# Token mixers with a shorter pipeline of steps, another step order, and gated keys copied by ScalarE

## The chip, the cores and the metric

The kernel runs on one core of a Trainium2 chip. The metric is the device time of one execution in microseconds; the median of three runs before the change is 2277.98 us (2274.43 to 2282.07).

## The reference

One inference step of a decoder with two layers, for a prompt of 512 tokens and for 8 samples of 8 tokens each (64 tokens), all in float32, width 1024. Per layer:

```
x += W_out @ concat(retention, gla, mlstm)(rmsnorm(x))      # 6, 6 and 4 heads, value width 64
x += memory_cross_attention(rmsnorm(x)); x += swiglu(rmsnorm(x))
# each mixer, in chunks of 128 tokens (8 for the samples):
o = (q k^T * decay) v + (q * q_decay) S ;  S = S * chunk_decay + (k * k_decay)^T v
# retention: fixed decays per head; gla: exp of a running sum of gates per channel;
# mlstm: exp of gate sums less a running maximum, and a normaliser as 65th value column
o = o * rsqrt(mean(o*o) + EPS) * gain * gate                 # per head and token
```

Every state is an output, of the prompt (starting from zero) and of the samples (starting from given states).

## The kernel before

**Units.** The large products stream weights. One unit is a block of 128 x 1024 of weights: a transfer (SyncE's queue) into `RAW`, an upper part `WH` by ScalarE (`upper`), the rest `WL` by GpSimd (`rests`), and 48 products on TensorE (`three`, L571): upper times upper, rest times upper and upper times rest, for two halves of 288 tokens and 8 blocks of the depth. The input is held so too, as `XH` and `XL`. After the output projection ("out") and after the projection of the cross attention ("xo"), `next_norm` adds each unit's sum to x (`add_to_x`, L1331), squares it, and behind the last unit writes all eight blocks of the next `XH` (ScalarE, `x_upper`) and `XL` (VectorE, `x_rest`, L1292); then come the sums of squares (L1302) and the statistics (L1308).

**The mixers.** Between the value projection and "out" stand 15 steps per layer, `STEPS`: for each chunk c of the prompt (0 to 3) and then for the samples (c = 4, written `NC` or S) the groups 0 (retention, three pairs of heads), 1 (gla, three) and 2 (mlstm, two). Step (1,2) is mlstm in chunk 1. Pairs of heads share the 128 partitions; in every prompt chunk the queries of the two heads are laid apart by ScalarE in `QE` (zero elsewhere). For step s TensorE runs `scores` (k q^T; for gla, `KG` holds keys with decays relative to four reference rows, 24 instructions of 64 columns), `keys` (transposes), `outputs` (the state's part from `QI` and `ST`, the values' part, and the new state's product into PSUM) and `back` (transposes of the normalised output). VectorE runs `mask_scores` (keys into `KTT`, scores times a mask into `SMX`), `take_outputs` (a copy of the outputs from PSUM to `OC`, L1695 and L1705), the sum of squares (L1784), the normalisation in place (L1799), `update_state` (mask the product L1718, scale the state L1727, add L1729), the gate (L1810), and for gla the decayed keys (a subtraction L1588 in `before`, a product L1602 in `before_end`). ScalarE lays queries apart, takes exponentials and squares `OC`; GpSimd makes the power -1/2 (L982, L986) and, for the samples, spreads values by sample (`own_values`, L253).

**Order.** Each engine's order is written out: TensorE in iteration i runs scores(i), back(i-3), keys(i), outputs(i-1). PSUM banks alternate by parity of the step. Engines are in order, and every hand-over is a semaphore. The states of the samples come by transfers that wait in SyncE's queue: `SC` and `SBD` (block-diagonal form) for three pairs at a time. In an `SBD` step 48 products and 12 of 512 columns stand on TensorE.

**Ahead of the steps** lies the gate arithmetic: a scan on VectorE (L1547), exponentials on ScalarE, GpSimd's clear of `QE` (L962) and its product for the decayed keys `KDG` (L965).

## Time and profile before

| | |
|---|---|
| median of 3 runs | 2277.98 us |
| profiled execution: time, span | 2289.77 us, 2287.8 us |
| mean granted clock of TensorE | 0.933 |
| mixers of layer 0, first scores to next projection | 314.5 to 475.2 us |
| mixers of layer 1 | 1437.2 to 1601.4 us |
| cross attention, feed-forward and projections | the rest, in both layers |

Times in the rows are microseconds from the start of the span, unless they are means in ns. PE is TensorE (PEld its weight loads), DVE VectorE, ACT ScalarE, POOL GpSimd.
### The profile page before, as it was taken

To read this page: it belongs to the slowest core of one execution; us is meant where nothing else is said; L and a number is where in the kernel's file an instruction comes from. 1 tells how busy PE (TensorE), PEld (TensorE's weight loads), DVE (VectorE), ACT (ScalarE), POOL (GpSimd) and SP (SyncE) were. 2 spreads that over 40 slices of the span, in tenths; PEclk is the share of its full clock that TensorE was granted. 3 is DMA by queue.
4 is the path that set the end of the run, shared out by engine and by line. 5 is a ranking of instruction groups with operands and counts; after the bars stand their busy time and mean duration, and the time that the engine had idled before them with its cause. 6 is when DMAs were issued, how large, how long until landed. Compare 5 with 4: busy or idle time off the path is not lost. (4 is left out here: it accounts for less than half of the span.)

```text
span 2287.8 us, 35847 instructions
## 1 busy us (share of the span) xinstructions
PE 2037.1 (89%) x14140; PEld 1908.2 (83%) x14140; DVE 938.2 (41%) x1301; ACT 626.3 (27%) x840; POOL 726.6 (32%) x356
## 2 busy tenths in 40 slices
PE   5999858689889999999799996786998999999995
PEld 5899647489679999999779984674994999999994
DVE  4543676624314330332173366774343243203313
ACT  4311542023323221222251126210323232212221
POOL 3333311323123334333343332122330233333331
PEclk9999967889999999999899997767999999999997
DMA  5432101225432222222343320013236122222221
GB/s 213 148 114 84 57 0 51 83 79 188 168 121 75 87 83 89 84 84 83 113 147 128 102 74 33 1 51 119 103 139 240 65 75 84 84 93 83 83 86 51
DMA packets 61270, 219.81 MB, mean 96 GB/s; under 512 B 10612, under 2 KB 11288, under 8 KB 58792
## 3 DMA queue, kind: packets, MB, share of 16 engines
q1 hardware_dynamic: 60216, 214.32, 26.1%
q10 hardware_dynamic: 880, 3.11, 0.4%
q8 instruction: 116, 1.90, 0.3%
q14 instruction: 58, 0.48, 0.1%
HBM read 202.47 MB, written 11.40 MB: 93 GB/s over the span
## 5 line engine op out<-in xcount | busy, mean ns | idle before, releaser
L954 POOL TENSOR_TENSOR WL<-RAW,WH 128x1024 fp32r<-128x1024 f32 (+1 forms) x276 | 645.1, 2337 | 1221.2 <-ACT WH L995 1221.2
L571 PE MATMUL PS<-XH,WH 128*128 128x288 f32 x2880 | 622.4, 298 | 18.4 <-DVE XL L1292 10.1
L571 PE MATMUL PS<-XH,WL 128*128 128x288 f32 x2880 | 618.9, 297 | 0.0
L571 PE MATMUL PS<-XL,WH 128*128 128x288 f32 x2880 | 618.9, 297 | 0.0
L995 ACT ACTIVATE WH<-RAW 128x1024 fp32r<-128x1024 f32 x276 | 292.3, 1059 | 1093.0 <-PE PS L571 1065.3
L571 PEld LDWEIGHTS PS<-XH,WH 128*128 128x128 f32 x2880 | 466.8, 190 | 24.1 <-issue 21.1
L571 PEld LDWEIGHTS PS<-XL,WH 128*128 128x128 f32 x2880 | 466.8, 190 | 0.0
L571 PEld LDWEIGHTS PS<-XH,WL 128*128 128x128 f32 x2880 | 466.8, 190 | 0.0
L571 PE MATMUL PS<-HH,WH 128*128 128x288 f32 x704 | 151.2, 296 | 4.1 <-DVE FT L1919 4.1
L571 PE MATMUL PS<-HH,WL 128*128 128x288 f32 x704 | 150.8, 296 | 0.0
L571 PE MATMUL PS<-HL,WH 128*128 128x288 f32 x704 | 150.7, 296 | 0.0
L1919 DVE TENSOR_TENSOR FT<-PS,RS 128x576 f32<-128x576 f32 x44 | 33.3, 758 | 235.9 <-PE PS L571 235.9
L1929 DVE TENSOR_TENSOR XT<-PS,XT 128x576 f32<-128x576 f32 x32 | 22.8, 752 | 251.5 <-PE PS L571 251.5
L571 PEld LDWEIGHTS PS<-HH,WH 128*128 128x128 f32 x704 | 113.3, 189 | 5.0 <-issue 5.0
L571 PEld LDWEIGHTS PS<-HH,WL 128*128 128x128 f32 x704 | 113.4, 189 | 0.0
L571 PEld LDWEIGHTS PS<-HL,WH 128*128 128x128 f32 x704 | 113.4, 189 | 0.0
L1926 DVE TENSOR_TENSOR HL<-FT,HH 128x576 fp32r<-128x576 f32 x44 | 93.2, 2118 | 33.3 <-ACT HH L995 33.3
L1331 DVE TENSOR_TENSOR XT<-PS,XT 128x576 f32<-128x576 f32 x32 | 24.2, 758 | 164.9 <-PE PS L571 164.9
L982 POOL TENSOR_SCALAR S<-S 128x6 f32<-128x6 f32 (+3 forms) x30 | 5.9, 198 | 213.6 <-DVE S L1784 213.6
L995 ACT ACTIVATE KTT<-OC 128x384 f32<-128x384 f32 (+3 forms) x30 | 14.6, 487 | 215.9 <-DVE OC L1695 129.5
L571 PE MATMUL PS<-MH,WH 128*128 128x256 f32 x128 | 39.6, 310 | 37.4 <-DVE ML L1345 33.5
L571 PE MATMUL PS<-QE,KT 128*128 128x256 f32 x80 | 25.0, 449 | 53.0 <-ACT QE L995 53.0
(259 smaller groups left out, 2474.7 us busy)
## 6 DMA issues: line engine op xcount, KB each, us to landing
RAW<-in_w_gu SPq DMA_DIRECT2D x88, 512.0 KB, 3.4
RAW<-in_w_dn SPq DMA_DIRECT2D x48, 512.0 KB, 3.4
RAW<-in_w_in SPq DMA_DIRECT2D x44, 512.0 KB, 3.5
KV<-in_cache_k SPq DMA_DIRECT2D x32, 512.0 KB, 7.1
KV<-in_cache_v SPq DMA_DIRECT2D x32, 512.0 KB, 7.3
RAW<-in_w_xk SPq DMA_DIRECT2D x16, 512.0 KB, 4.6
RAW<-in_w_xv SPq DMA_DIRECT2D x16, 512.0 KB, 3.4
RAW<-in_w_v SPq DMA_DIRECT2D x16, 512.0 KB, 3.4
```

The lines of the kernel that those rows point to most:

```text
L571: return nc.tensor.matmul(out, lhsT=lhsT, rhs=rhs, start=start, stop=stop)
L954: nc.gpsimd.tensor_tensor(WL[:, s, w], RAW[:, r, w], WH[:, s, w].bitcast(f32), ALU.subtract).then_inc(split_done.sem, 1)
L982: nc.gpsimd.tensor_scalar(small("ms", n, par)[0:L], small("ss", n, par)[0:L], 1.0 / 64, EPS, ALU.mult, ALU.add).then_inc(pool_step.sem, po ...
L995: return nc.scalar.activation(out, in_, func, **kw)
L1331: tt(two(XT[:, b, :]), halves(b % 2), two(XT[:, b, :]), ALU.add).then_inc(gemm_evac.sem, 1)
L1919: tt(two(FT[:, 2 + b % 2, :]), halves(1), two(RS[:, :]), ALU.mult).then_inc(gemm_evac.sem, 1)
L1926: tt(HL[:, b, :], FT[:, 2 + b % 2, :], HH[:, b, :].bitcast(f32), ALU.subtract).then_inc(hl_ready.sem, 1)
L1929: tt(two(XT[:, b, :]), halves(b % 4), two(XT[:, b, :]), ALU.add).then_inc(gemm_evac.sem, 1)
```

## The change

- **Step order.** The 15 steps run (0,0) (0,1) (1,0) (1,1) (2,0) (2,1) (3,0) (3,1) (0,2) (S,0) (1,2) (S,1) (2,2) (3,2) (S,2).
- **Shorter pipeline.** TensorE in iteration i runs scores(i+1), keys(i+1), back(i-2), the new `new_state(i)` (the state's product, taken out of `outputs`), outputs(i). `back` lies two steps behind instead of three.
- **Outputs.** No copy to `OC` first: ScalarE squares the outputs from PSUM, VectorE sums the squares (`mean_squares`, with EPS, formerly GpSimd's) before the next mask, and `take_outputs` normalises straight from PSUM. The mlstm division by the normaliser, and retention's query decay, are common factors of a row of outputs: they are left out and EPS is scaled instead (`EPSR`); retention's mask is built by ScalarE (`RD`, `RDS`) without them.
- **Retention scores** use half of the partitions per head, without `QE`. Chunk 0 has no product with the state.
- **State.** Two buffers `ST[0]`, `ST[1]`: ScalarE writes the scaled state into the other one (`scale_state`), VectorE adds the halves of the product.
- **Decayed keys.** The subtraction is gone; ScalarE takes twelve exponentials of 128 elements with the reference as bias. The transposed gated keys are copied to `KTT` by ScalarE (`take_decayed_keys`).
- **Samples.** ScalarE spreads the values (`spread_values`), GpSimd clears two query tiles `QB`.
- **Transfers.** `SC` is loaded right after the gate arithmetic, `SBD` for the first three pairs after the transposes of (3,1), for the second three after the products of (S,0), `SBDM` after those of (S,1), `SCM` after the transposes of (3,2). Their order in SyncE's queue stays otherwise; the store of the first `SC` still stands ahead of its second load.
- **Projections.** In the last unit of "out" and "xo" TensorE signals each block of `XH`/`XL` that it is done with (`x_free`), and `next_norm` writes the next one at once, seven of eight before the last sum.

The diff's core:

```diff
-STEPS = [(c, g) for c in range(NC + 1) for g in range(3)]
+STEPS = [(0, 0), (0, 1), (1, 0), (1, 1), (2, 0), (2, 1), (3, 0), (3, 1),
+         (0, 2), (NC, 0), (1, 2), (NC, 1), (2, 2), (3, 2), (NC, 2)]
+AT = {step: n for n, step in enumerate(STEPS)}
+APART = [n for n, (c, g) in enumerate(STEPS) if c < NC and g > 0]
+UNDECAYED = [n for n, (c, g) in enumerate(STEPS) if g != 1]
+SCALED = [n for n, (c, g) in enumerate(STEPS) if 0 < c < NC]
+GAMMA = [1.0 - 2.0 ** (-5.0 - h) for h in range(6)]
...
-        ST = sb("ST", [128, PAIRS, 130])
...
+        QB = [place("QB0", [128, 3, 576], r_kk), place("QB1", [128, 3, 576], r_xh)]
...
+                            if frees and b == stop - 1 and k < KB - 1:
+                                last.then_inc(x_free.sem, 1)
...
+                        if s in APART:
+                            both = bank(q + p // 2, 256 * (p % 2), 256).rearrange("p (e i) -> p e i", e=2)
+                            slot = APART.index(s) % 2
+                            if grp == 2:
+                                mm(both, KT[:, p0 + p, t0:t0 + L], QE[:, slot, p, :, :], True, True)
+                                continue
                             for i in range(4):
                                 w = slice(32 * i, 32 * i + 32)
-                                mm(both[:, :, w], KG[:, p, i, :], QE[:, s % 2, p, :, w], True, True)
-                        elif c < NC:
-                            mm(both, KT[:, p0 + p, t0:t0 + L], QE[:, s % 2, p, :, :], True, True)
-                        else:
-                            for e in range(2):
-                                r = slice(64 * e, 64 * e + 64)
-                                k = KGS[r, p, :] if grp == 1 else KT[r, p0 + p, t0:t0 + L]
-                                mm(bank(q + e, CH * p, L)[0:L], k, QT[r, p0 + p, t0:t0 + L], True, True)
+                                mm(both[:, :, w], KG[:, p, i, :], QE[:, slot, p, :, w], True, True)
+                            continue
...
+                def new_state(s):
...
+                    if c == NC:
+                        pe.wait_ge(sm_ready.sem, sm_ready.at(l, s + 1))
+                        pe.wait_ge(vb_ready.sem, vb_ready.at(l, grp + 1))
+                    stand_alone(pe)
+                    for p in range(n):
+                        if c < NC:
+                            last = mm(bank(q + 2, 2 * W * p, 2 * W), KTT[:, par, 128 * p:128 * p + 128],
+                                      V[:, c, value_at(grp, p, 0, W):value_at(grp, p, 0, W) + 2 * W], True, True)
+                            continue
+                        for e in range(2):
+                            k = KTT[0:64, par, 128 * p + 64 * e:128 * p + 64 * e + 64]
+                            last = mm(bank(q + p)[64 * e:64 * e + 64], k, own_values(grp)[:, 2 * p + e, :], True, True)
...
+                    last.then_inc(u_done.sem, 1)
...
+                        pe.wait_ge(gated.sem, gated.at(l, s - 1))
...
+                        if 0 < c < NC:
+                            queries = (QT if grp == 0 else QI)[:, p0 + p, t0:t0 + L]
+                            mm(o2, queries, state(c % 2, p0 + p, 1)[:, 0, 0:2 * W], True, False)
...
-                for i in range(len(STEPS) + 3):
+                scores(0)
+                keys(0)
+                for i in range(len(STEPS) + 2):
+                    if i + 1 < len(STEPS):
+                        scores(i + 1)
+                        keys(i + 1)
+                    if i >= 2:
+                        back(i - 2)
                     if i < len(STEPS):
-                        scores(i)
-                    if 3 <= i:
-                        back(i - 3, i)
-                    if i < len(STEPS):
-                        keys(i)
-                    if 1 <= i <= len(STEPS):
-                        outputs(i - 1)
+                        new_state(i)
+                        outputs(i)
...
+                nc.gpsimd.memset(QB[1][:, :, :], 0.0).then_inc(qb_zero.sem, 1)
...
+                nc.gpsimd.tensor_tensor(KDG[:, :, 0:SEQ], KDG[:, :, 0:SEQ], KT[:, 3:6, 0:SEQ], ALU.mult).then_inc(kdg_ready.sem, 1)
+                nc.gpsimd.tensor_tensor(KDS[:, :, :], KDG[:, :, SEQ:NT], KT[:, 3:6, SEQ:NT], ALU.mult).then_inc(kdg_ready.sem, 1)
...
-                    act.wait_ge(unit_done.sem, unit_done.at(l, U0[stage] + 8))
                     for k in range(KB - 1):
+                        act.wait_ge(x_free.sem, x_free.at(l, (KB - 1) * (n - 1) + k + 1))
                         x_upper(name, k)
-                        if k == 2:
-                            upper(stage, 7 + SPLIT_SLOTS)
+                    upper(stage, 7 + SPLIT_SLOTS)
...
+                def decay_keys(c):
+
+                    if c == 0:
+                        act.wait_ge(ga_used.sem, ga_used.at(l, 1))
+                    else:
+                        act.wait_ge(ma_done.sem, ma_done.at(l, AT[c - 1, 1] + 1))
+                    for p in range(3):
+                        for i in range(4):
+                            last = do(KG[:, p, i, :], GB[:, p, CH * c:CH * c + CH], ACT.Exp, scale=-1.0 / 16,
+                                      bias=small("gref", 1, 16 * p + 4 * c + i))
+                    last.then_inc(kg_exp.sem, 1)
...
+                def scale_state(s):
+
+                    if s in SCALED:
+                        c, grp = STEPS[s]
+                        p0, n = GROUPS[grp]
+                        act.wait_ge(st_done.sem, st_done.at(l, AT[c - 1, grp] + 1))
+                        act.wait_ge(mb_done.sem, mb_done.at(l, AT[c - 1, grp] + 1))
...
+                        for p in range(n):
...
+                            last = do(state((c + 1) % 2, p0 + p, 1)[:, 0, :], state(c % 2, p0 + p, 1)[:, 0, :], ACT.Copy, scale=decay)
+                        last.then_inc(st_scaled.sem, 1)
+
+                def take_decayed_keys(s):
+
+                    c, grp = STEPS[s]
+                    if grp == 1:
+                        L = chunk_of(c)[1]
+                        if s >= 2:
+                            act.wait_ge(u_done.sem, u_done.at(l, s - 1))
+                            act.wait_ge(ss_ready.sem, ss_ready.at(l, s - 1))
+                        act.wait_ge(ma_done.sem, ma_done.at(l, s + 1))
+                        do(KTT[0:L, s % 2, 0:384], bank(4 * (s % 2) + 2, 0, 384)[0:L], ACT.Copy).then_inc(kg_taken.sem, 1)
+
+                def spread_values(grp, half):
+
...
+                    for b in range(4 * half, 4 * half + 4):
+                        last = do(own_values(grp)[:, :, 64 * b:64 * b + 64], v, ACT.Copy,
+                                  scale=COLS[0:64, COL["batch"] + b:COL["batch"] + b + 1])
+                    if half == 1:
+                        last.then_inc(vb_ready.sem, 1)
+
+                decay_keys(0)
                 act.wait_ge(qe_zero.sem, qe_zero.at(l, 1))
                 act.wait_ge(g_ready.sem, g_ready.at(l, 1))
...
+                for i in range(len(STEPS)):
+                    c, grp = STEPS[i]
+                    n, L = GROUPS[grp][1], chunk_of(c)[1]
+                    queries_apart(i + 2)
+                    if grp == 2:
                         act.wait_ge(dm_ready.sem, dm_ready.at(l, c + 1))
                         d = SMX[0:L, i % 2, 0:512].rearrange("p (q i) -> p q i", q=4)[:, :, 0:L]
                         do(d, d, ACT.Exp).then_inc(dexp_ready.sem, 1)
...
+                    if grp == 1 and c + 1 < NC:
+                        decay_keys(c + 1)
+                    scale_state(i)
+                    if i + 1 < len(STEPS):
+                        take_decayed_keys(i + 1)
+                    act.wait_ge(mb_done.sem, mb_done.at(l, i + 1))
+                    w = 65 if grp == 2 else 64
+                    do(KTT[0:L, i % 2, 0:128 * n].rearrange("p (h v) -> p h v", h=2 * n),
+                       bank(4 * (i % 2) + 3, 0, 2 * n * w)[0:L].rearrange("p (h v) -> p h v", h=2 * n)[:, :, 0:64],
+                       ACT.Square).then_inc(sqo_ready.sem, 1)
+                    for g, before in ((0, AT[NC - 1, 1]), (1, AT[NC, 0]), (2, AT[2, 2])):
+                        if before <= i < before + 2:
+                            spread_values(g, i - before)
...
                 def next_norm(n, name, stage):
 
-                    for b in range(KB):
+                    for b in range(KB - 1):
                         add_to_x(stage, b)
                         if b >= 1:
                             add_square(l, sq_ready, sq_used, n, b - 1)
                     for k in range(KB - 1):
                         x_rest(n, name, k)
+                    add_to_x(stage, KB - 1)
                     x_rest(n, name, KB - 1)
+                    add_square(l, sq_ready, sq_used, n, KB - 2)
                     add_square(l, sq_ready, sq_used, n, KB - 1)
                     rms(n)
 
@@ -1499,27 +1607,13 @@
...
+                def decayed_keys(c):
+
+                    dve.wait_ge(kg_exp.sem, kg_exp.at(l, c + 1))
+                    for p in range(3):
+                        last = stt(KG[:, p, :, :], KG[:, p, :, :], CAP,
+                                   spread(KT[:, 3 + p, CH * c:CH * c + CH], [128, 4, CH], 1), ALU.min, ALU.mult)
+                        if p < 2:
+                            last.then_inc(dve_step.sem, dve_step.tick())
+                    last.then_inc(kg_ready.sem, 1)
...
+                def take_keys(s):
...
+                def mean_squares(s):
+
+                    c, grp = STEPS[s]
+                    n, L, par = 2 * GROUPS[grp][1], chunk_of(c)[1], s % 2
+                    ss, ms = small("ss", n, 6 * par)[0:L], small("ms", n, 6 * par)[0:L]
+                    dve.wait_ge(sqo_ready.sem, sqo_ready.at(l, s + 1))
+                    V_.tensor_reduce(ss, KTT[0:L, par, 0:64 * n].rearrange("p (h v) -> p h v", h=n),
+                                     AX.X, ALU.add).then_inc(dve_step.sem, dve_step.tick())
...
+                    dve.wait_ge(pw_ready.sem, pw_ready.at(l, s + 1))
+                    tt(OC[0:L, par, 0:64 * n].rearrange("p (h v) -> p h v", h=n),
+                       bank(4 * par + 3, 0, w * n)[0:L].rearrange("p (h v) -> p h v", h=n)[:, :, 0:64],
+                       spread(small("pw", n, 6 * par)[0:L], [L, n, 64], 2), ALU.mult).then_inc(on_ready.sem, 1)
...
+                        u = bank(q + 2, 0, 2 * W * n).rearrange("p (q w) -> p q w", q=n)
+                        for e in range(2):
+                            r, w = slice(64 * e, 64 * e + 64), slice(W * e, W * e + W)
+                            st = state((c + 1) % 2, p0, n)[r, :, w]
+                            last = tt(st, st, u[r, :, w], ALU.add) if c > 0 else V_.tensor_copy(st, u[r, :, w])
+                            if e == 0:
+                                last.then_inc(dve_step.sem, dve_step.tick())
+                        last.then_inc(st_done.sem, 1)
...
+                for i in range(N + 2):
+                    if i < N and STEPS[i][1] == 2:
+                        exponents_masked(i)
+                    if 1 <= i <= N:
+                        update_state(i - 1)
+                        mean_squares(i - 1)
                     if i < N:
+                        if STEPS[i][1] != 1:
+                            take_keys(i)
                         mask_scores(i)
+                    if i >= 2:
+                        gate(i - 2)
                     if 1 <= i <= N:
                         take_outputs(i - 1)
+                    if i < N and STEPS[i][1] == 1 and STEPS[i][0] + 1 < NC:
+                        decayed_keys(STEPS[i][0] + 1)
+                    if i + 2 < N and STEPS[i + 2][1] == 2:
+                        row_operand(STEPS[i + 2][0])
+                    if i + 1 < N and STEPS[i + 1][0] == NC:
+                        sample_operands(STEPS[i + 1][1])
```

## Rows read from the trace of the kernel before

**Rows 1.** The page's first part: busy us (share) and instructions of each engine.
```profile
PE 2037.1 (89%) x14140; PEld 1908.2 (83%) x14140; DVE 938.2 (41%) x1301; ACT 626.3 (27%) x840; POOL 726.6 (32%) x356
```
**Rows 2.** Busy table by stretches: window, length, busy (x instructions), granted clock, DMA, GB/s.
```profile
314.50:475.20 160.70, 117.91 (x715) 99.74 (x715) 101.76 (x195) 26.18 (x49) 35.46 (x36) 0.78 0.17 61
...
1437.20:1601.40 164.20, 124.89 (x714) 106.07 (x715) 99.93 (x194) 25.91 (x48) 35.45 (x36) 0.74 0.17 60
...
1534.00:1592.10 58.10, 39.34 (x253) 30.69 (x251) 26.05 (x46) 1.88 (x4) 19.98 (x14) 0.74 0.27 91
...
1592.10:1601.40 9.30, 0.81 (x5) 0.55 (x6) 6.32 (x16) 2.08 (x4) 1.19 (x2) 0.67 0.46 164
...
1451.00:1458.50 7.50, 4.06 (x28) 3.22 (x27) 5.35 (x11) 4.37 (x7) 1.53 (x2) 1.00 0.00 0
...
1458.50:1470.00 11.50, 11.50 (x63) 11.50 (x61) 8.25 (x18) 1.14 (x3) 2.73 (x4) 0.55 0.00 0
...
1483.00:1502.50 19.50, 19.50 (x81) 17.31 (x80) 13.07 (x28) 1.66 (x4) 2.73 (x4) 0.50 0.00 0
```
**Rows 3.** Time line of TensorE, prompt steps: start, us, operation [idle before <-releaser].
```profile
1478.31 1.53 PE L571 MATMUL PS<-QE,KT 128*128 128x256 f32 x6 [1.39 <-ACT QE L995]
...
1481.17 0.52 PE L808 MATMUL PS<-IDENT,OC 128*128 128x128 f32 x3 [1.32 <-DVE OC L1799]
...
1482.69 0.87 PE L754 MATMUL PS<-IDENT,KT 128*128 128x128 f32 x3 [1.00 <-DVE ST L1729]
...
1530.71 0.56 PE L571 MATMUL PS<-QT,KT 64*64 64x64 f32 x12
```
**Rows 4.** Time line of TensorE, the sample steps.
```profile
1542.87 0.87 PE L808 MATMUL PS<-IDENT,OC 128*128 128x128 f32 x3 [4.83 <-DVE OC L1799]
...
1562.95 0.66 PE L571 MATMUL PS<-RHS,ROWS 36*64 36x256 f32 x1 [7.44 <-DVE SC L1737]
...
1578.76 0.56 PE L808 MATMUL PS<-IDENT,OC 64*128 64x64 f32 x3 [2.66 <-DVE OC L1799]
...
1582.83 3.70 PE L571 MATMUL PS<-SBDM,QB 128*64 128x130 f32 x16 [3.52 <-DVE GT L1810]
```
**Rows 5.** Time line ahead of the first step of layer 1.
```profile
1395.43 0.69 ACT L995 ACTIVATE R<-R 4x576 f32<-4x576 f32 x1 [5.77 <-DVE R L1498]
...
1420.62 1.61 DVE L1558 COPY S<-GB 128x12 f32<-128x12 f32 x3
...
1420.84 0.35 ACT L995 ACTIVATE KGS<-GB 128x192 f32<-128x192 f32 x1
...
1428.23 3.82 POOL L965 TENSOR_TENSOR KDG<-KDG,KT 128x1728 f32<-128x1728 f32 x1 [6.02 <-ACT KDG L995]
...
1428.28 5.52 DVE L1588 TENSOR_TENSOR KG<-S,GB 128x512 f32<-128x512 f32 x3
```
**Rows 6.** Groups by form, 1437 to 1602 us: busy us, mean ns, idle before <-releaser.
```profile
L1588 DVE TENSOR_TENSOR KG<-S,GB 128x512 f32<-128x512 f32 x9 | 5.7, 683 | 0.0
...
L1672 DVE TENSOR_TENSOR SMX<-PS,CMASK 128x768 f32<-128x768 f32 x4 | 3.8, 950 | 0.0
...
L1718 DVE TENSOR_TENSOR SMX<-PS,COLS 128x384 f32<-128x384 f32 x8 | 4.4, 549 | 0.0
...
L995 ACT ACTIVATE QE<-QT 64x384 f32<-64x384 f32 x15 | 7.7, 516 | 0.1
...
L995 ACT ACTIVATE KG<-KG 128x1536 f32<-128x1536 f32 x3 | 4.4, 1483 | 10.0 <-DVE KG L1588 10.0
```
**Rows 7.** Time line at layer 1's output projection: block sums, statistics, TensorE's next.
```profile
1648.31 0.76 DVE L1331 TENSOR_TENSOR XT<-PS,XT 128x576 f32<-128x576 f32 x1 [4.98 <-PE PS L571]
...
1654.71 0.76 DVE L1331 TENSOR_TENSOR XT<-PS,XT 128x576 f32<-128x576 f32 x1 [4.97 <-PE PS L571]
...
1666.50 0.76 DVE L1308 TENSOR_SCALAR RS<-PS 128x576 f32<-128x576 f32 x1 [1.73 <-PE PS L571]
...
1657.00 0.82 PE L571 MATMUL PS<-XH,WH 128*128 128x288 f32 x2 [2.33 <-DVE XL L1292]
```

More of the change, by code:

```diff
@@ L412, in prompt_state @@
         def prompt_state(p0, n, w, half):
[L414 removed]
+            return state(0, p0, n)[64 * half:64 * half + 64, :, w * half:w * half + w]
         @block.sync
@@ L1112, in _ @@
                 upper("v", 6)
+                act.wait_ge(masks_loaded.sem, 4 * 16)
+                for h in range(6):
+                    do(RD[:, h, :], CMASK[:, :], ACT.Copy, scale=KDI[:, h:h + 1])
+                    last = do(RDS[:, h, :], CMASKS[:, :], ACT.Copy, scale=KDI[0:64, 6 + h:7 + h])
+                last.then_inc(rd_ready.sem, 1)
                 act.wait_ge(f_ready.sem, f_ready.at(l, 1))
@@ L1284, in _ @@
             dve.wait_ge(const_loaded.sem, const_loaded.at(0, 64))
+            for h in range(6):
+                for at, name, steps in ((h, "kd", CH), (6 + h, "kds", DEC_S)):
+                    ts(KDI[:, at:at + 1], COLS[:, COL[name] + h:COL[name] + h + 1], GAMMA[h] ** -steps, None,
+                       ALU.mult).then_inc(dve_step.sem, 1)
+            dve.wait_ge(dve_step.sem, 14)
+            stt(EPSR[:, :], KDI[:, :], EPS, KDI[:, :], ALU.mult, ALU.mult).then_inc(dve_step.sem, 1)
             with dve.Fori(0, DEPTH) as l:
@@ L1579, in _ @@
                 N = len(STEPS)
-                def before(s):
-                    if s < N and STEPS[s][1] == 1 and STEPS[s][0] < NC:
-                        c = STEPS[s][0]
-                        if s >= 3:
-                            dve.wait_ge(ma_done.sem, ma_done.at(l, s - 2))
-                        for p in range(3):
-                            last = tt(KG[:, p, :, :], spread(gref[:, p, c, :], [128, 4, CH], 2),
-                                      spread(GB[:, p, CH * c:CH * c + CH], [128, 4, CH], 1), ALU.subtract)
-                            if p < 2:
-                                last.then_inc(dve_step.sem, dve_step.tick())
-                        last.then_inc(pre_sub.sem, 1)
```

489 lines of the change are left out of this document (212 added, 277 removed).

## The prediction

> **What bounds the kernel now.** The page's busy shares come first: TensorE is busy 89% of the span [rows 1], so time is to be gained only where TensorE pauses or runs at half clock. The busy table by stretches says where: in the mixers, 160.7 and 164.2 us in the two layers. TensorE is busy 117.9 and 124.9 us in them, at mean clocks 0.78 and 0.74 [rows 2]. The product is 92 us both times: that is the work at full clock. The rest of a layer's mixers is 39 to 43 us of pauses and 26 to 33 us lost to half clock. VectorE, with 100 to 102 us busy, is the next engine. The time line then shows the pauses. In a chunk of the prompt TensorE stops 1.39, 1.32 and 1.00 us, for queries that ScalarE copies, for normalised outputs and for the state sum on VectorE [rows 3], with small ones 4.0 us a chunk. The clock follows: 7.5 us with 4.06 busy at full clock, then 11.5 us at half; another stretch of half clock is 19.5 us long [rows 2]. The sample steps stand together at the end, 58.1 us with 39.3 busy [rows 2], behind pauses of 4.83, 7.44, 2.66 and 3.52 us [rows 4]. Last is a tail of 9.3 us from the last products to the next projection, with TensorE 0.8 busy [rows 2].
>
> **The change part by part.** All is for one layer at full clock, unless said.
>
> *Ahead of the steps.* VectorE loses the subtraction for the decayed keys: 5.52 us with GpSimd's product beside it [rows 5], of which three instructions of 0.68 (as their like in [rows 6]) are its own 2.0. The other 3.5 is the hindrance by GpSimd's product (3.82), which stays and now meets VectorE's product of queries and decays. GpSimd also clears a second query tile, as large as the one whose clear stood beside VectorE's three tiny copies of 1.61 [rows 5]: 1.5 more, or 0 if it meets nothing. Net 0.5, bounds 0 and 2. ScalarE's twelve scaled mask copies, 12 x 0.3 = 3.6, fall into its wait of 5.77 [rows 5]; without that cover they are 3.6 late. Chunk 0 skips eight products with a zero state (0.14 each by the time line's pitch, 1.2). I take 2 gained.
>
> *VectorE per step.* The plain copy of the outputs, the scaling of the state and its masking go, 0.55 each [rows 6]; the state's sum becomes two half-height, half-width instructions (0.35 each, between half of 0.55 and the whole), and the gated group's transposed keys (0.55) go to ScalarE. VectorE had about 20 us a chunk (100 less some 20 in the sample steps, over four) and gets 14; TensorE has 15.8 ((92 - 39.3 x 0.74) / 4). VectorE's volume no longer bounds, its place in the chain may.
>
> *The new cycle in the prompt.* From the end of a step's products to the start of the next: ScalarE's square 0.52, VectorE's reduction 0.55, a small sum 0.2, mask 0.95, gate 0.55, and with retention keys 0.55 [rows 6]: 2.8 to 3.3 us. Beside it TensorE has the next scores, six transposes and the state product, 2.9 to 4.5 us, so this wait is nearly covered. What is late is ScalarE. In a gated step it takes the square 0.52, queries 2 x 0.52, and then twelve exponentials of 128 elements in place of one of 1536 in 1.48. No row shows that size; from 192 elements in 0.35 and 1536 in 1.48 [rows 5, 6] the slope is 0.84 ns an element and 128 take 0.30: 3.6 in all (bounds 12 x 0.23 = 2.8, and 12 x 0.35 = 4.2). Exponentials end 5.2 us after the retention step's products; VectorE multiplies them, 3 x 0.6; the next gated scores can start at 7.1, and TensorE is free at 5.0. So it pauses 2.1 for each such pair, three times, with 2 at the start 8 us. Before, four chunks paused 16. Gain 8. Behind the exponentials in ScalarE's queue stand three scalings of the state (0.9) and the square, for which VectorE's mask waits: no more than TensorE's 4.5 beside it. If they do come last, 1 us a pair.
>
> *The last seven steps.* The sample steps now lie between mLSTM chunks, with scores one step ahead. ScalarE is in order again: behind a square come four copies that spread sample values, 4 x 0.52, a query copy 0.8, and the exponential 0.6 (128 x 512 by the slope above); then VectorE's keys 0.4, mask 0.7, gate 0.5. Ahead of the products of (0,2) and (1,2) that is 5.7 us against 1.6 of other work: two pauses of 4.2. (2,2) has none, (3,2) 2.0, the last sample step 3.6. Sum 14, against 18.5 in [rows 4]: gain 4. The block-diagonal states are issued a step ahead, and their landing is covered by some 10 us of TensorE's work; I take nothing, and 2 to 5 lost if the second pair's store and load in turn (SP's queue waits for the store) come late.
>
> *Tail.* Square from PSUM 0.4, reduction 0.4, four small sums 0.8, power 1.0, normalise 0.4, transpose 0.45, gate 0.3, split 1.5, semaphores 0.8: 6 against 9.3, 3 gained.
>
> *Clock.* The pauses give 2 + 8 + 4 + 3 = 17, of which I take 12, as the chains leave out semaphore waits (0.1 to 0.2 each, some 30 on the path). Half clock cost 26 to 33. There will be fewer pauses in the prompt, but two of 4 us remain, of the size after which the clock fell. I take it that two of the long stretches (11.5 and 19.5 us, each costing half its length) go or are shorter: 12 gained, bounds 0 and 26. A layer: 24.
>
> A rule speaks against this. The Trainium skill (TensorE: Matmul & The Clock Gate, A second HAM failure mode: psum-queue depth-cycling) says that frequent micro-idles between groups of products make the clock swing, with no long pause needed. The trace agrees: the clock fell behind pauses of 1.0 to 1.4 us [rows 2, 3]. By this rule alone the clock's 12 would be 0 and the time 24 later.
>
> Retention scores are now half-height products, twelve for six. Twelve of 64x64 take 0.56 and six of 256 columns 1.53 [rows 3]; so one to two times 0.56 for twice the columns, 0.4 to 1 less a step, which I leave in the bounds. The Trainium skill (TensorEngine Tiling (Array Packing), Key Properties) says that such tiles run in parallel, but that a change of the tiling mode drains the engine: by the second half, these few tenths are given back at each change.
>
> *At the output projections.* The first seven blocks of the next normalised input are now written during the last unit, as TensorE frees them. Before, TensorE waited 2.33 us for the first block and then ran at the pace of VectorE's blocks; from the last block's sum to the statistics' there passed 11.8 us [rows 7], where a unit is 6.4 (the pitch of the sums) and the statistics 1.2. Saved 4.0, four times (two places, two layers): 16. VectorE was idle 4.97 us of that unit [rows 7], which hides seven blocks of 1.0 for the most part. The last block (sum, upper, rest: 0.76 + 0.7 + 1.1) is there before TensorE has done the other seven eighths of a unit.
>
> **Sum.** 2 x 24 + 16 = 64. The profiled execution took 2289.8 (span 2287.8); the median of the runs shown is 2278.0, 11.8 below. 2289.8 - 64 = 2225.8, and as a median 2214.
>
> **The rivals.**
> A. *The clock stays full.* Of the half clock only 3 a layer are left: 2 x (12 + 27) + 16 = 94, median 2184. For it: pauses in the prompt halve. Against: those of 4 us. 0.22.
> B. *The pauses only move.* ScalarE's order, the square behind exponentials and spreads, costs what VectorE's did; left are the tail and some of the interleave, 2 x 8 + 16 = 32, median 2246. For it: ScalarE was 26 us busy of 164 [rows 2] and now gets over 150 short instructions. 0.14.
> C. *Slower: the clock collapses.* With a pause at every step TensorE stays at half clock. 92 us of work at mean clock c and 20 of pauses that slow work doesn't cover meet the 162.5 of now, plus 8 from the projections, at 92/c = 150, c = 0.61. At 0.55 it is 187 a layer, 17 above that point: 34 more, median 2312. 0.04.
> D. *The input isn't written early*, because frees come late or GpSimd's subtraction slows the blocks: the 16 are gone, median 2230. It is inside the forecast's share, with 0.05.
>
> The forecast has 0.58, and 0.02 is for a stall that I don't see. The range takes in A and B with the bounds above: 2178 to 2250. A measurement of this kernel tells 0.3% (7 us) from no change. Faster 0.93, same 0.03, slower 0.04.
>
> **What would show it.** Mixers of about 138 us, first scores to next projection, at a mean clock above 0.82. In the prompt, TensorE's longest waits stand ahead of the products of queries and decayed keys, are released by VectorE, and last 2 us, three a layer. Waits of about 4 us ahead of (0,2) and (1,2). No wait for the first block at a projection. ScalarE's exponentials at 0.3 each. It is wrong if the mean clock stays as it was, if a DMA releases the longest pauses, or if VectorE is still busy over 95 us in a layer's mixers.

## The result

| | before | after |
|---|---|---|
| median of all runs | 2276.2 us (2270.3 to 2282.1) | 2247.05 us (2243.99 to 2253.96, 4 runs) |
| ratio | | 0.9876, 95% interval 0.9841 to 0.9911 |
| profiled execution | 2289.8 us | 2244.0 us |
| mean granted clock of TensorE | 0.933 | 0.936 |
| mixers, layers 0 and 1 | 160.7 and 164.2 us | 147.6 and 148.2 us |

The change makes the kernel 28 us faster by the ratio (1.2%); 64 were forecast. Between the two profiled executions the difference is 46 us, because that of before was 12 above its median and that of after 3 below its own. It splits into 13 + 16 in the mixers, 6 in the stretch ahead of them (two layers), some 9 at the projections and 2 elsewhere.

### The profile page after: what moved, and what is told of

Same layout as the page of the kernel before. It is cut to its first block, busy times and chain, and to the rows that moved or that the text cites. A ratio compares the mean times of both kernels' runs of the same rounds, so it can differ in the third digit from the quotient of the medians.

```text
span 2241.9 us, 36034 instructions
## 1 busy us (share of the span) xinstructions
PE 2033.2 (91%) x14156; PEld 1897.3 (85%) x14156; DVE 881.0 (39%) x1244; ACT 682.1 (30%) x1042; POOL 700.7 (31%) x320
## 4 chain that ended last, share of the span: by engine, by line
PE 78%; DVE 7%; ACT 6%; issue 4%; DMA 2%; SPq 1%; POOL 1%; ACTq 0%; DVEq 0%; POOLq 0%
PE PS L591 77%; DVE XL L1398 1%; ACT KG L1032 1%; DMA KV<-in_cache_k 1%; DMA KV<-in_cache_v 1%; DVE CY L1556 1%; ACT WH L1032 1%; SPq L566 1%; POOL WL L999 1%; ACT QT L1032 1%; DVE RS L1408 1%; ACT XH L1032 1%; ACT QE L1032 0%; PE PS L782 0%; ACT V L1032 0%
## 5 line engine op out<-in xcount | busy, mean ns | idle before, releaser
L1023 POOL TENSOR_TENSOR S<-S,MHALF 128x6 f32<-128x6 f32 (+3 forms) x30 | 36.5, 1216 | 254.6 <-DVE S L1792 106.9
L1032 ACT ACTIVATE KTT<-PS 128x384 f32<-128x384 f32 (+3 forms) x40 | 18.4, 459 | 189.8 <-PE PS L591 144.4
L591 PE MATMUL PS<-WH,XH 128*128 128x512 f32 x160 | 63.9, 400 | 7.1 <-POOL WL L999 3.8
```

The source lines that it names most:

```text
L591: return nc.tensor.matmul(out, lhsT=lhsT, rhs=rhs, start=start, stop=stop)
L1023: nc.gpsimd.tensor_tensor(small("pw", n, par)[0:L], small("ms", n, par)[0:L], MHALF[0:L, 0:n], ALU.pow).then_inc(pw_ready.sem, 1)
L1032: return nc.scalar.activation(out, in_, func, **kw)
```

## The profile after

The page's first part after, answering to [rows 1]. VectorE has 57 us less, ScalarE 56 more, and TensorE's busy share is higher:

```profile
PE 2033.2 (91%) x14156; PEld 1897.3 (85%) x14156; DVE 881.0 (39%) x1244; ACT 682.1 (30%) x1042; POOL 700.7 (31%) x320
```

The busy table of after answers to [rows 2]: first the mixers of both layers, then one clock swing of layer 1, which begins in a pause.

```profile
core 0: us, PE busy (x) PEld busy (x) DVE busy (x) ACT busy (x) POOL busy (x), PEclk, DMA share, GB/s
310.50:458.10 147.60, 122.70 (x722) 101.08 (x722) 73.11 (x170) 49.12 (x128) 19.73 (x16) 0.73 0.21 67
1412.30:1560.50 148.20, 121.49 (x722) 99.55 (x722) 73.17 (x170) 49.14 (x128) 19.73 (x16) 0.74 0.21 67
...
1443.60:1447.90 4.30, 2.19 (x18) 2.07 (x18) 2.57 (x5) 4.30 (x15) 0.00 (x0) 1.00 0.00 0
...
1449.50:1456.00 6.50, 6.50 (x33) 6.50 (x33) 2.97 (x7) 0.49 (x1) 1.22 (x1) 0.50 0.01 3
1456.00:1462.40 6.40, 5.88 (x54) 5.40 (x53) 2.70 (x5) 4.98 (x16) 1.32 (x1) 1.00 0.00 0
```

Read each mixer row in three parts. Length less PE busy is idle time: 25 and 27 us, where before had 43 and 39. Busy time by the mean clock is, roughly, the work at full clock: 90 us both times, 92 before. The rest of the busy time, 33 and 32 us, is what half clock cost, and before it was 26 and 33. The mean clock of a row counts the pauses too, so this split is a rough one. Added up over only those stretches that the trace has at 0.50, half clock costs 36 and 34 us now and 26 and 34 before, and the work at full clock is 87 us in both layers, 92 and 91 before. So the pauses went, by more than was forecast, and the clock gave nothing back: in layer 0 it took 10 more.

TensorE's time line of layer 1, every row with a pause above 1 us behind the first scores, answers to [rows 3, 4]:

```profile
1430.60 5.35 PE L591 MATMUL PS<-QE,KG 128*128 128x64 f32 x24 [3.46 <-DVE KG L1681]
...
1447.93 4.19 PE L591 MATMUL PS<-QE,KG 128*128 128x64 f32 x24 [2.12 <-DVE KG L1681]
...
1464.65 3.86 PE L591 MATMUL PS<-QE,KG 128*128 128x64 f32 x24 [2.23 <-ACT QE L1032]
...
1484.23 1.21 PE L591 MATMUL PS<-V,KTT 128*128 128x130 f32 x4 [3.36 <-DVE KTT L1735]
...
1507.14 1.11 PE L591 MATMUL PS<-V,KTT 128*128 128x130 f32 x4 [3.61 <-DVE KTT L1735]
...
1537.40 0.69 PE L591 MATMUL PS<-V,KTT 128*128 128x130 f32 x4 [1.11 <-DVE KTT L1735]
...
1544.91 1.98 PE L591 MATMUL PS<-QT,KTT 64*64 64x512 f32 x4 [3.33 <-DVE SMX L1764]
...
1558.11 0.31 PE L851 MATMUL PS<-IDENT,OC 64*128 64x64 f32 x2 [2.90 <-DVE OC L1805]
...
1560.54 0.82 PE L591 MATMUL PS<-XH,WH 128*128 128x288 f32 x2 [2.11 <-DVE XL L1906]
```

Why the pause at 1447.93 is there, from the time line of ScalarE and VectorE: ScalarE's square of the outputs and its two copies of the queries come first, the twelve exponentials only then, and VectorE waits 1.73 for the last of them. The third such pause, at 1464.65, is put down to a query copy of ScalarE; that copy ends at 1464.45, and VectorE's products of the gated keys end only just before it, at 1464.39.

```profile
1440.79 0.49 ACT L1032 ACTIVATE KTT<-PS 128x384 f32<-128x384 f32 x1 [3.67 <-PE PS L591]
...
1441.17 1.04 ACT L1032 ACTIVATE QE<-QT 64x384 f32<-64x384 f32 x2
...
1442.24 3.62 ACT L1032 ACTIVATE KG<-GB,S 128x128 f32<-128x128 f32 x12
...
1445.89 1.90 DVE L1681 SCALAR_TENSOR_TENSOR KG<-KG,KT 128x512 f32<-128x512 f32 x3 [1.73 <-ACT KG L1032]
```

## The experiments

All are edits of the changed kernel, and each was compared with the kernel before on the same chip (medians of before 2276.8, 2275.3 and 2273.6 in the three groups). The changed kernel itself was not run again in these groups, so a difference from it, or between groups, goes by way of the ratios to before; by their intervals such a difference is uncertain by 9 to 14 us. A profiled execution says where the time is; medians say how much. Theory P: pauses of 2 us and more bring half clock, and the half clock behind them costs as much as they do. Theory W: the work itself runs at half clock. The other parts of the change (outputs normalised straight from PSUM, two state buffers, scores on half the partitions) were not tried one by one.

**Unread products in the pauses.** TensorE multiplies the identity by itself where it would wait; nobody reads the result. The second kernel has them only ahead of the first step, the third in both places.

```diff
+ def fill(n, s, half=False):      # n products of 128 columns into an unused corner
# scores, group 1, ahead of its waits:
+     fill({1: 10, 2: 6, 3: 6}.get(c, 0), s)
# new_state, ahead of its waits:
+     fill({8: 11, 10: 11, 13: 3, 14: 10}.get(s, 0), s if c == NC else s + 1, True)
# ahead of the first step, behind the wait for the keys' exponentials:
+ fill(20, 0)
```

> The changed kernel, and in its seven pauses of TensorE a layer products that nothing reads: 10, 6, 6 of 128 columns ahead of the gated scores of chunks 1 to 3, and 11, 11, 3, 10 ahead of the state products of (0,2), (1,2), (3,2) and (S,2). Theory P (the pauses bring the half clock: each of 2 to 3.6 us is followed by 6.5 to 15 us at half clock, some 55 us a layer): the mixers' mean clock rises from 0.73 to above 0.9, a layer's mixers fall from 148 to 125 or less, and the kernel is 30 to 50 us faster than the changed one (about 2205). Rival W (the clock falls because of the work itself, small products and 64-column scores, pause or not): clock stays at 0.70 to 0.76, the time within 5 us of the changed kernel's 2247, or some us more for the added products.

> The changed kernel with 20 products of 128 columns that nothing reads on TensorE ahead of the first step, from the end of ScalarE's exponential for the decayed keys on, where TensorE waited 20.4 us. Theory P: the first steps, now 10 us at half clock, start at full clock; 4 to 5 us a layer, 8 to 10 us faster than the changed kernel (about 2238). Rival W: the clock falls within the first steps anyway: 0 to 3 us.

> Both sets of unread products. Theory P: the gains add up, 40 to 60 us less than the changed kernel (2190 to 2205), mixers at 118 to 125 us a layer with a mean clock above 0.93. Rival W: within 5 us of the changed kernel.

Measured: in the pauses 2204.7 (ratio 0.9693, 0.9641 to 0.9745), ahead of the steps 2243.1 (0.9845, 0.9796 to 0.9893), both 2195.2 (0.9632, 0.9584 to 0.9681). The products in the pauses do work for nobody and take 42 us off. The mixers take 124 and 131 us, where the theory had 125 or less. The busy table of that kernel's mixers:

```profile
310.20:434.60 124.40, 109.61 (x836) 93.23 (x836) 72.96 (x170) 49.10 (x128) 19.71 (x16) 0.94 0.24 79
1388.10:1519.30 131.20, 116.42 (x836) 96.57 (x836) 72.83 (x170) 49.08 (x128) 19.70 (x16) 0.89 0.23 75
```

The clock is 0.94 and 0.89 where it was 0.73 and 0.74, with all useful products still there. So most of the half clock comes with the pauses, as P says, and W falls as the account of the 33 us a layer. P is not the whole of it, though. In layer 1 of this kernel 13.6 us at half clock (1474.0 to 1487.6) follow a pause of only 1.07, and the same pause in layer 0 is followed by none. With the products in both places, layer 1 of the profiled execution has 13.7 us at half clock with no pause above 1 us in the 46 us before. The lines are the two longest pauses just ahead of it and then the stretch itself, in which TensorE is busy 13.54 us:

```profile
1447.48 0.68 PE L591 MATMUL PS<-V,KTT 128*128 128x130 f32 x4 [0.81 <-DVE KTT L1748]
1448.63 1.08 PE L591 MATMUL PS<-V,SMX 128*128 128x65 f32 x8 [0.46 <-DVE GT L1890]
...
1449.80:1463.50 13.70, 13.54 (x38) 7.18 (x39) 6.46 (x17) 2.34 (x5) 1.01 (x1) 0.50 0.01 1
```

What brings these stretches is open. Ahead of the first step the products are worth 4 us alone and 9.5 on top of the others; neither is clear of the noise.

**The projections' tail as before.** Blocks of the next input are written only behind the last unit again.

```diff
# TensorE: units "out" and "xo" without frees=True
# ScalarE: ahead of the blocks
-   act.wait_ge(x_free.sem, ...)     # per block
+   act.wait_ge(unit_done.sem, unit_done.at(l, U0[stage] + 8))
# VectorE: all eight add_to_x and squares first, then all x_rest
```

> The changed kernel with the projections' tail as before: the next normalised input is written only after the last unit, in four places. From the profile of the changed kernel (9.6 us from the end of the last unit to the statistics, 11.8 before) it should be 4 x 2.2 = 9 us slower than the changed kernel, about 2256. If the early writing gained the 4.0 us a place that the prediction took: 16 us slower, 2263. If something else in the transition gave the 2.2 us: no difference.

Measured: 2253.5 (0.9898, 0.985 to 0.995), 6.5 us above the changed kernel, where the forecast gave this part 16. The medians alone do not tell 6.5 from 0 or from 16. The profiles do tell: in all four places the time from the last unit's end to the statistics is 11.8 us again, and 9.6 in the changed kernel, so the part is worth four times 2.2.

**The step order of before.** STEPS runs chunk by chunk again, the samples last; the clear of the query tile and the spreading of the sample values move with it. All else is as changed.

```diff
-STEPS = [(0, 0), (0, 1), (1, 0), (1, 1), (2, 0), (2, 1), (3, 0), (3, 1),
-         (0, 2), (NC, 0), (1, 2), (NC, 1), (2, 2), (3, 2), (NC, 2)]
+STEPS = [(c, g) for c in range(NC + 1) for g in range(3)]
```

> The changed kernel with the step order of before (chunk by chunk, the sample steps last), everything else as changed. Theory: the order itself is part of the gain, since sample steps that stand together bare their waits. In the changed kernel the last seven steps hold pauses of 3.4, 3.6, 1.1 and 3.3 us; with the old order I expect the four of before again, 16 to 18 us instead of 11.4, and 4 to 6 us more at half clock a layer: 18 to 25 us in all, a median of 2265 to 2272. Rival: ScalarE's and VectorE's work per step sets the pauses, not the neighbours, and the interleave only moved them: 2244 to 2252.

Measured: 2215.2 (0.9734, 0.9694 to 0.9774). I had expected this kernel 18 to 25 us slower, and it is 32 us faster: theory and rival both missed. The new order is the part of the change that costs. TensorE's time line of layer 1 in this kernel, every pause above 1 us but the one ahead of the first step:

```profile
1423.71 0.69 PE L590 MATMUL PS<-V,KTT 128*128 128x130 f32 x4 [1.15 <-DVE KTT L1734]
...
1439.50 0.52 PE L781 MATMUL PS<-IDENT,KT 128*128 128x128 f32 x3 [1.17 <-DVE ST L1823]
...
1456.99 0.52 PE L781 MATMUL PS<-IDENT,KT 128*128 128x128 f32 x3 [1.17 <-DVE ST L1823]
...
1476.20 0.69 PE L590 MATMUL PS<-V,KTT 128*128 128x130 f32 x4 [2.49 <-DVE KTT L1734]
...
1499.09 2.79 PE L590 MATMUL PS<-KT,KTT 64*64 64x512 f32 x12 [1.46 <-ACT KT L1031]
...
1503.98 1.93 PE L590 MATMUL PS<-SBD,QB 128*64 128x128 f32 x16 [2.09 <-DMA SBD<-in_sbd]
...
1515.82 1.89 PE L590 MATMUL PS<-QT,KTT 64*64 64x512 f32 x4 [4.69 <-DVE SMX L1763]
...
1529.11 0.30 PE L850 MATMUL PS<-IDENT,OC 64*128 64x64 f32 x2 [2.93 <-DVE OC L1804]
...
1531.52 0.82 PE L590 MATMUL PS<-XH,WH 128*128 128x288 f32 x2 [2.11 <-DVE XL L1905]
```

and its busy table, both layers' mixers, then layer 1's beginning, the prompt from there to its end, and the next 15 us:

```profile
311.20:441.50 130.30, 109.20 (x723) 90.75 (x723) 72.66 (x170) 49.50 (x128) 19.74 (x16) 0.83 0.24 76
1401.20:1531.50 130.30, 107.70 (x722) 88.01 (x723) 72.66 (x170) 49.46 (x128) 19.73 (x16) 0.84 0.23 76
...
1401.20:1421.20 20.00, 20.00 (x92) 17.62 (x94) 9.83 (x19) 6.63 (x19) 1.32 (x1) 0.52 0.13 40
1421.20:1478.00 56.80, 48.10 (x388) 42.32 (x387) 42.43 (x101) 29.50 (x81) 13.77 (x11) 1.00 0.08 29
1478.00:1493.00 15.00, 14.36 (x69) 9.27 (x69) 6.23 (x17) 4.80 (x10) 1.01 (x1) 0.54 0.01 2
```

A layer's mixers take 130.3 us against 148. Idle time is 21 and 23 us (25 and 27 in the new order), half clock costs 19 and 17 (33 and 32, all by the mean clock). So 14 of the 17 to 18 us a layer are clock. Layer 0 has one more pause than the lines show, 2.34 us ahead of transposes that wait for VectorE's state (329.78), and half clock behind it. Ahead of the gated scores there is no pause above 1 us now in either layer: in the chunk of this row the exponentials start at 1450.07 and VectorE's products end at 1455.59, while TensorE takes up the gated scores only at 1460.74. A chunk has a third step, the mlstm one, between them.

```profile
1450.07 3.60 ACT L1031 ACTIVATE KG<-GB,S 128x128 f32<-128x128 f32 x12
...
1453.70 1.89 DVE L1680 SCALAR_TENSOR_TENSOR KG<-KG,KT 128x512 f32<-128x512 f32 x3 [0.58 <-ACT KG L1031]
...
1460.74 1.50 PE L590 MATMUL PS<-QE,KG 128*128 128x64 f32 x12
```

**The transposed gated keys copied by VectorE again.**

```diff
# take_keys, VectorE, in all gated steps; take_decayed_keys (ScalarE) is not called
+   if grp == 1:
+       V_.tensor_copy(kt, bank(q + 2, 0, 384)[0:L]).then_inc(kg_taken.sem, 1)
```

> The changed kernel with the gated group's transposed keys copied by VectorE again (0.55 us, five a layer) in place of ScalarE. Theory: in a gated step both engines have room beside TensorE's work, so the copy is off the path either way: 0 to 4 us, a median of 2245 to 2251. Rival: the copy stands in VectorE's chain ahead of the mask for which the outputs wait, and five of them a layer cost 0.5 each and some half clock: 2255 to 2262.

Measured: 2243.5 (0.9864, 0.9842 to 0.9886), just under the theory's range and not distinct from the changed kernel. Which engine copies these keys makes no difference that these runs can tell.

**The exponentials handed on by head pairs**, once in the changed kernel and once together with the order of before.

```diff
# ScalarE, decay_keys: one signal behind each four exponentials, not behind twelve
-                    last.then_inc(kg_exp.sem, 1)
+                        last.then_inc(kg_exp.sem, 1)
# VectorE, decayed_keys: likewise, a wait and a signal for each pair
# TensorE, scores of group 1, inside the loop over pairs:
+   if p > 0:
+       pe.wait_ge(kg_ready.sem, kg_ready.at(l, 3 * c + p + 1))
```

> The changed kernel, with ScalarE's twelve exponentials of a gated chunk handed on after each four (one head pair) instead of after all twelve, VectorE's three products likewise, and TensorE's products of queries and decayed keys waiting pair by pair. Theory (the exponentials set the three pauses of 2.1 to 3.5 us a layer): the pauses lose 1.2 us or more each, with 3.6 to 6 us a layer gone, and some of the half clock behind them (up to 3 us each): a median of 2222 to 2240. Rival (the square and the scalings in ScalarE's queue, or VectorE's queue, set them): pauses of 2 us stay, 2243 to 2248.

> Both edits in one: the step order of before, and the exponentials handed on by head pairs. By themselves they gave 32 us (order of before) and 26 us (hand-over) against the changed kernel. Theory: in the order of before a gated chunk's exponentials lie beside the mLSTM step and the next retention step, so nothing waits for them, and the hand-over has nothing left to give: 2210 to 2218. Rival: the two repair different things and add up: 2185 to 2195.

Measured: 2221.3 (0.9768, 0.9746 to 0.979) in the new order, 26 us less than without; 2214.4 (0.9719, 0.9685 to 0.9753) with the order of before, 1 less than without. The second theory held and its rival, that the gains add up, did not: the two repair the same thing. TensorE's time line of layer 1 with the hand-over in the new order, its first two pauses above 1 us since the first step, and its busy table up to the first of them:

```profile
1462.95 0.69 PE L591 MATMUL PS<-V,KTT 128*128 128x130 f32 x4 [3.36 <-DVE KTT L1736]
...
1485.17 1.20 PE L591 MATMUL PS<-V,KTT 128*128 128x130 f32 x4 [3.61 <-DVE KTT L1736]
```

```profile
1406.60:1422.60 16.00, 15.40 (x102) 14.72 (x103) 7.30 (x14) 6.46 (x19) 1.32 (x1) 0.70 0.16 50
1422.60:1462.90 40.30, 34.30 (x292) 31.11 (x291) 29.16 (x63) 23.20 (x66) 10.73 (x8) 1.00 0.12 40
1462.90:1538.00 75.10, 60.82 (x330) 42.59 (x331) 36.54 (x94) 19.43 (x45) 7.65 (x7) 0.73 0.31 99
```

The three pauses (3.46, 2.12, 2.23) are gone, and the clock stays full for 40 us.

**Only the end mixed.** The order of before for chunks 0 and 1, then the steps of the diff.

```diff
+STEPS = [(0, 0), (0, 1), (0, 2), (1, 0), (1, 1), (1, 2), (2, 0), (2, 1), (3, 0), (3, 1),
+         (2, 2), (NC, 0), (3, 2), (NC, 1), (NC, 2)]
```

> The order of before for chunks 0 to 2, and only the end mixed: (2,0), (2,1), (3,0), (3,1), (2,2), (S,0), (3,2), (S,1), (S,2). Theory: what the changed kernel's order costs lies in the three pairs without an mLSTM step between them; here one such pair is left (a pause of 2 to 3 us and 3 to 5 of half clock), and the end gains 2 to 4 by the mixing. So near the order of before: 2213 to 2226. Rival: mixing the sample steps with mLSTM steps is what costs (pauses of 3.4 and 3.6 us before (0,2) and (1,2)): 2230 to 2245.

Measured: 2228.2 (0.9792, 0.9748 to 0.9835), between the two: above the theory's range, which ended at 2226, and under the rival's, which began at 2230. The one pair without an mlstm step between brings its pause back, and mlstm steps with a sample step beside them theirs:

```profile
1466.01 4.88 PE L591 MATMUL PS<-QE,KG 128*128 128x64 f32 x24 [2.37 <-ACT QE L1032]
...
1485.59 0.69 PE L591 MATMUL PS<-V,KTT 128*128 128x130 f32 x4 [3.36 <-DVE KTT L1735]
...
1507.44 1.17 PE L591 MATMUL PS<-V,KTT 128*128 128x130 f32 x4 [2.75 <-DVE KTT L1735]
```

Both places have their pauses. The run is 13 us above the order of before, which is about the uncertainty of that difference, and it does not share them out between the places.

**How far filling goes.** Unread products in the mixers' tail, on top of the kernel of 2195.2; and with the order of before, ahead of the first step alone, and in its pauses too.

```diff
# 2195.2's kernel: back(14) and the wait of the first unit
+ fill(20, 1)
+ fill(13, 1)
# the order of before: ahead of the first step, then also in the pauses
+ fill(20, 0)
+ fill({1: 3}.get(c, 0), s)                                   # scores, group 1
+ fill({11: 8, 13: 5, 14: 12}.get(s, 0), ..., True)           # new_state
```

> The kernel with unread products in the pauses and ahead of the first step (2195.2 before), and now 20 and 13 unread products more in the two waits of the mixers' tail (2.90 and 2.11 us). Theory: the tail is the last pause behind which the clock halves; the first 5 to 8 us of the output projection then run at full clock, 2.5 to 4 us a layer: a median of 2187 to 2191. Rival: the projection's dense work brings the clock back at once and the tail costs its own length only: 2194 to 2197.

> The order of before in the changed kernel, and 20 unread products of 128 columns on TensorE ahead of the first step. In the order of before the first 20 us of the mixers run at half clock although they hold no pause above 1.2 us, and then 56 us at full. Theory: the half clock there comes from the 20 us of idling before the steps, so the products bring full clock forward by 6 to 10 us: 3 to 5 a layer, a median of 2205 to 2209. Rival: as with the order of the changed kernel, where they gave 4 in all, small pauses undo it: 2211 to 2216.

> As the kernel with the order of before and the 20 products ahead of the steps, and unread products also in its pauses: 3 ahead of the gated scores of chunk 1, 8 ahead of the state product of (3,2), 5 and 12 ahead of those of the second and third sample step. Theory: the half clock behind the pauses of 2.5 and 4.7 us goes, 4 to 8 us a layer: a median of 2190 to 2200, so the order of before is as good as the changed order with all pauses filled (2195), or better. Rival: the sample steps' half clock comes from their products of half height, not from pauses: 2205 to 2212.

Measured: tail 2206.6 (0.9705, 0.9674 to 0.9735), above both forecasts, so nothing shows that the tail's pauses are worth filling; I can't say whether it does harm. Ahead of the first step 2216.0 (0.9723, 0.969 to 0.9756), nothing, as the rival said. In layer 1 the clock is full earlier, TensorE comes early to a state that VectorE hasn't written, pauses 2.34 (to 1422.35), and 10 us at half clock follow. Layer 0 had that pause already without these products. In the pauses too 2204.1 (0.9686, 0.9649 to 0.9722): between the two expectations. The busy table of the kernel with the products ahead only:

```profile
1401.00:1411.00 10.00, 9.67 (x67) 9.46 (x67) 8.93 (x11) 5.68 (x17) 3.99 (x2) 0.72 0.25 78
1411.00:1421.00 10.00, 9.01 (x73) 7.78 (x72) 6.03 (x12) 6.02 (x17) 1.32 (x1) 1.00 0.01 2
1421.00:1431.00 10.00, 8.16 (x40) 7.71 (x40) 6.99 (x19) 2.72 (x7) 2.33 (x2) 0.64 0.01 2
```

The fastest kernel of the study is the changed one with unread products in its pauses and ahead of its steps, 2195.2, 52 us under the changed kernel. Of the versions without such products, the order of before with everything else changed: 2215.2, or 2214.4 with the hand-over.

## Why the prediction was wrong

- **What failed: the clock, 12 a layer.** "I take it that two of the long stretches go or are shorter." Half clock costs 36 and 34 us a layer after, 26 and 34 before (counted over the stretches at 0.50): not one of the 12 came, and layer 0 lost 10 more. The mean clock of the mixers is 0.73 and 0.74, where I had said above 0.82 and had named a clock that stays as it was as a sign of being wrong. For the profiled execution 2225.8 was forecast and 2244.0 came, 18 later. The clock missed by 34 (24 and 10) and the projections by 7. Against that the pauses gave 36 (30 in the mixers, 6 ahead of them) where I had 24, the work at full clock fell by 8, most of which I had left in the bounds, and some 2 came elsewhere. The other 15 us between 2214 and 2247 are the step from that execution to the median: I took 11.8 off, as before, and the profiled execution of after lies 3 below its median. I had counted pauses by their sum, and the clock goes by their size and place. My own working had three pauses of 2.1 in the prompt and two of 4.2 behind it; they came as 3.46, 2.12, 2.23 and 3.36, 3.61. A pause of 2.12 is followed by 6.5 us at half clock (1449.5 to 1456), the one of 3.61 by 17.1 (1507.2 to 1524.3). With the seven pauses filled 42 us went. I should have priced each forecast pause of 2 us or more with half clock behind it.
- **The rule that spoke against it** gave a time 24 later, 2238; measured 2247. The Trainium skill (TensorE: Matmul & The Clock Gate, A second HAM failure mode: psum-queue depth-cycling) names short idles between groups of products as a cause for a clock that swings. The traces agree with the direction, and the 24 us were worked out from my own terms, not from the page. How short an idle may be is left open by this section and by these runs: with the order of before, pauses of 1.15 and 1.17 us left the clock full for 56.8 us (until just behind one of 2.49), while in the kernel before half clock came behind three of 1.0 to 1.4 within 6 us [rows 2, 3], and in the kernels with unread products behind one of 1.07 and one of 0.81.
- **The new cycle in the prompt.** Its mechanism is right and shown: three waits of 2.1 to 3.5 ahead of the products of queries and decayed keys, exponentials that follow each other at 0.30 (3.62 for twelve), and all three waits gone when the exponentials are handed on by pairs. What I did not do was to ask what the old order would have given with the same instructions. It hides these waits wholly; the new order turned a covered wait into three pauses. The order costs 32 us in all, the last seven steps included.
- **The last seven steps.** 4.2, 4.2, 0, 2.0 and 3.6 were forecast; 3.36, 3.61, 0, 1.11 and 3.33 came, with a sum of 11.4 for 14. But the price of mixing (half clock behind the first two) was left out. The remark that I take nothing for the transfers held: none releases a pause in the new order; in the order of before, `SBD` costs 2.09.
- **Tail.** 5.6 us against 9.3 (1554.9 to 1560.5), 2.90 and 2.11 of it the last two waits; 6 was worked out.
- **Retention scores.** 0.94 us a step at full clock against 1.53 in [rows 3]: 0.6 less, inside the 0.4 to 1 that I left in the bounds. No run shows what the change between half-height and full products costs.
- **Ahead of the steps.** From the gates' first product to the first scores 33.5 us in each layer against 36.2 and 36.4: 2.7 and 2.9 less, where I had 2 with the zero state's products. GpSimd's clear did not hold VectorE up: 0 of the 1.5. The hindrance by GpSimd's product stayed, but it met another instruction than I had worked out: a copy of 128 x 192 that took 0.28 before takes 3.42 beside it, and the product of queries and decays keeps its 1.73.
- **Projections, 4.0 four times.** Mis-sized. From the last unit's end to the statistics it takes 9.6 us now against 11.8 in [rows 7], in all four places: 2.2 saved each, 9 in all, and undoing it cost 6.5 by the medians. The seven blocks of `XL` take VectorE 7 x 1.21 = 8.5 us of a unit in which it was idle for 4.97; I called that hidden for the most part. So the last block's sum starts only 4.4 us after the unit's end. The time line of after: ScalarE's next split at the unit's end, that sum, the statistics:

```profile
1614.12 1.06 ACT L1032 ACTIVATE WH<-RAW 128x1024 fp32r<-128x1024 f32 x1
...
1618.47 0.74 DVE L1439 TENSOR_TENSOR XT<-PS,XT 128x576 f32<-128x576 f32 x1
...
1623.73 0.76 DVE L1414 TENSOR_SCALAR RS<-PS 128x576 f32<-128x576 f32 x1 [1.33 <-PE PS L591]
```

The group of the blocks, between 1600 and 1632 us, with the mean in ns:

```profile
L1398 DVE SCALAR_TENSOR_TENSOR XL<-XT,VECS,XH 128x576 fp32r<-128x576 f32 x8 | 9.3, 1218 | 1.8 <-ACT XH L1032 1.8
```

- **The rivals.** B (pauses only move, 2246) has the measured time, but not by its mechanism: the idle time did shrink, by 18 and 13 us. A and C did not happen, and D (input not written early) neither, though its place delivered only 2.2 of the 4.0.
- With the order of before the rest of the change gives 60 us, near the 64 of the forecast. That is no proof of it: its mixers lose 30 and 34 us, where I had 24, and its projections 2.2 each, where I had 4.

## What to carry to other kernels

When TensorE shares its time with waits, don't add the waits up: list each, and as an estimate count every one of 2 us or more a second time for half clock behind it (here 2.12 was followed by 6.5 us at half clock, which cost 3.3, and 3.61 by 17.1, which cost 8.6). Waits near 1 us can go either way: some left the clock full and some did not, and only the trace of the kernel at hand tells. Before a new order of steps is priced, put the same instructions into the old one and see which wait it covers: an order that hides a 5 us chain of ScalarE and VectorE behind one more step was worth more here than all the interleaving of samples. And to learn what half clock costs in a kernel, fill the pauses with products nobody reads: if the time falls, it was the clock; if it doesn't, nothing is shown.

## What the hardware showed that I had not expected

- 57 short unread products a layer, 3 to 11 in a place, take 42 us off the kernel.
- Beginning after 20 us without products, TensorE was busy for 19.2 us without a pause at half clock before full clock came (order of before, layer 1, 1401.2 to 1420.4). In layer 0 of the same execution, with the same instructions, it took 10.1 us (311.2 to 321.3). So neither the order nor the work makes this difference; what does was not tried.
- Half clock also came with no pause above 1 us in the 46 us before: 13.7 us of it, with TensorE busy 13.54, in the kernel with unread products in both places.
- In the order of before, where full clock came early (layer 0, and layer 1 with products ahead of its steps), TensorE met a pause of 2.34 us for a state of VectorE's, and half clock for 10 us came behind it. Where full clock came late (layer 1 without them) there was no such pause.
